# Splitting projection weights one piece further ahead in a two-block transformer kernel

## The reference, cut to what matters

```
u = rmsnorm(h, norm_mix[i]) @ w_mix_in[i]
z, xbc, dt_raw, q, k, v, q_idx, k_idx, w_idx = split(u)
y_ssd = ssd_mixer(z, xbc, dt_raw, ...)      # 16 heads of a state-space mixer
y_att = dsa_mixer(q, k, v, q_idx, k_idx, w_idx, positions)  # 8 heads, top 64 keys of an indexer
h = h + concat(y_ssd, y_att) @ w_mix_out[i]
```

## Time and profile before

| | |
|---|---|
| median of three runs | 2865.03 us |
| the profiled execution | 2873.32 us, its span 2871.5 us |
| PE busy | 2749.1 us, 96% of the span |
| DVE, ACT, POOL busy | 65%, 45%, 14% |
| mean granted TensorE clock | 0.976 of full speed |
| moved by DMA | 445.24 MB, mean 155 GB/s |

### The profile page before, as it was taken

How to read it: one execution, slowest core, us unless ns; L and a number is a source line. 1 busy time by engine, 2 the same in 40 slices (tenths; PEclk the granted TensorE clock), 3 DMA queues, 4 the chain that set the end, 5 groups by cost and what they waited for, 6 DMA issues and landing times.

```text
span 2871.5 us, 40240 instructions
## 1 busy us (share of the span) xinstructions
PE 2749.1 (96%) x17078; PEld 2334.2 (81%) x17078; DVE 1877.0 (65%) x2495; ACT 1284.3 (45%) x1603; POOL 392.3 (14%) x331
## 2 busy tenths in 40 slices
PE   7999998999999999899999999999999979999998
PEld 6889877888888977788888765768878868889787
DVE  7856467685775546678599643347757659654774
ACT  5433535444444344554433544524444433665443
POOL 2400010231230001023004311010000001411000
PEclk9998999999999899999999999999999999999999
DMA  7563694455554479255423221235545524334652
GB/s 230 183 194 108 219 288 154 147 187 188 168 183 155 148 232 298 91 183 186 146 74 101 82 70 61 69 106 188 184 161 183 185 68 147 99 119 126 211 184 96
DMA packets 442329, 445.24 MB, mean 155 GB/s; under 512 B 13711, under 2 KB 433672, under 8 KB 442150
## 3 DMA queue, kind: packets, MB, share of 16 engines
q1 hardware_dynamic: 438878, 436.52, 47.6%
q0 software_dynamic: 2400, 5.40, 0.8%
q10 hardware_dynamic: 872, 0.75, 0.1%
HBM read 441.46 MB, written 1.17 MB: 154 GB/s over the span
## 4 chain that ended last, share of the span: by engine, by line
PE 88%; DVE 7%; ACT 3%; DMA 1%; issue 1%; SPq 0%; ACTq 0%; DVEq 0%
PE bank L1655 30%; PE bank L1617 19%; PE bank L1656 15%; PE bank L1609 7%; PE bank L1754 4%; PE bank L1650 2%; DVE R L2723 2%; PE bank L1871 2%; PE bank L2079 1%; PE bank L1812 1%; PE bank L2070 1%; DVE lower L2230 1%; DVE lower L724 1%; PE bank L1941 1%; ACT upper L1084 1%
## 5 line engine op out<-in xcount | busy, mean ns | idle before, releaser
L1655 PE MATMUL bank<-h_pair,upper 128*128 128x512 f32 x2464 | 877.0, 400 | 31.9 <-DVE h_pair L2263 18.7
L2230 DVE TENSOR_TENSOR lower<-ring,upper 128x2048 fp32r<-128x2048 f32 (+1 forms) x238 | 567.2, 2385 | 291.2 <-ACT upper L1084 291.1
L1656 PE MATMUL bank<-h_pair,lower 128*128 128x256 f32 x2464 | 694.5, 282 | 0.0
L1084 ACT ACTIVATE upper<-ring 128x2048 fp32r<-128x2048 f32 (+1 forms) x238 | 441.7, 1863 | 484.2 <-PE bank L1656 482.9
L1655 PEld LDWEIGHTS bank<-h_pair,upper 128*128 128x128 f32 x2464 | 467.4, 190 | 147.9 <-issue 29.3
L1656 PEld LDWEIGHTS bank<-h_pair,lower 128*128 128x128 f32 x2464 | 470.3, 191 | 0.2
L1655 PE MATMUL bank<-hid_pair,upper 128*128 128x512 f32 x1232 | 432.7, 396 | 0.0
L1656 PE MATMUL bank<-hid_pair,lower 128*128 128x256 f32 x1232 | 344.9, 280 | 0.0
L1655 PEld LDWEIGHTS bank<-hid_pair,upper 128*128 128x128 f32 x1232 | 231.1, 188 | 55.2
L717 DVE TENSOR_TENSOR lower<-ring,upper 128x2048 fp32r<-128x2048 f32 (+1 forms) x68 | 149.2, 2196 | 167.5 <-ACT upper L1050 167.5
L1617 PE MATMUL bank<-h_up,upper 128*128 128x512 f32 (+1 forms) x640 | 227.2, 355 | 20.3 <-DVE h_low L2677 19.0
(11 more groups left out here) (334 smaller groups left out, 4566.1 us busy)
## 6 DMA issues: line engine op xcount, KB each, us to landing
ring<-in_w_ffn_in SPq DMA_DIRECT2D x154, 1024.0 KB, 5.1
ring<-in_w_ffn_out SPq DMA_DIRECT2D x56, 1024.0 KB, 4.9
ring<-in_w_mix_in SPq DMA_DIRECT2D x48, 1024.0 KB, 5.4
ring<-in_w_mod SPq DMA_DIRECT2D x48, 1024.0 KB, 6.7
ring<-in_w_in SPq DMA_DIRECT2D x42, 1024.0 KB, 5.2
ring<-in_w_ffn_out SPq DMA_DIRECT2D x28, 768.0 KB, 4.2
ring<-in_w_mix_out SPq DMA_DIRECT2D x16, 1024.0 KB, 5.8
ring<-in_w_in SPq DMA_DIRECT2D x16, 512.0 KB, 5.2
```

The costliest lines, as they stand in the source:

```text
L1084: act.activation(f.upper(p)[:, 0:n], slot[:, 0:n], ACT.Copy).then_inc(up_ready, 1)
L1655: pe.matmul(bank[:, 0:2 * T], up[:, cols], x_pair.rearrange("p e t -> p (e t)"), start=first, stop=False)
L1656: return pe.matmul(bank[:, 0:T], low[:, cols], x_pair[:, 0, :], start=False, stop=last)
L2230: dve.tensor_tensor(f.lower(p)[:, 0:n], slot[:, 0:n], f.upper(p)[:, 0:n].bitcast(F32), ALU.subtract)\
```

## The change

Uppers and lowers of the qkv pieces are made two pieces ahead instead of one. On ACT piece n + 2 is split right after the result of piece n has been copied out; before, piece n + 1 was split just before waiting for piece n. Piece 1 is now split after the last piece of z. On DVE the lowers follow, and in the pairs they stand on the other side of the decay rows (L2582). The first piece of the output projection is split on ACT before the squares and roots, not between the two roots, and on DVE before the reciprocals, not in attention step 3. What PE and SyncE run, and in which order, stays as it was.

```diff
                     if i == 0:
                         split1_up(mixp + 13)
-                    elif i == 2:
-                        split1_up(poss + FILL_PIECE["qkv", 0])
+                    elif i >= 2:
+                        split1_up(poss + FILL_PIECE["qkv", i - 2])
 
                 def take_fills(kind, i):
                     for what, n in FILLS.get((kind, i), ()):
                         it = items + FILL_ITEM[what, n]
-                        if what == "qkv" and n + 1 < len(QKV_AT):
-                            split1_up(poss + FILL_PIECE[what, n + 1])
                         filled(act, it)
                         if what == "qkv":
                             take_item(it, [(qkv[:, :, PC * n:PC * (n + 1)], token_halves(banks(it)[0]))])
+                            if n + 2 < len(QKV_AT):
+                                split1_up(poss + FILL_PIECE[what, n + 2])
...
+                split1_up(poss + MIXO_PIECE)
                 for gr in range(2):
                     act.wait_ge(y_gated, (l * KD + 4 * (gr + 1)))
...
                                    scale=2.0 / D).then_inc(yroot_ready, 1)
-                    if gr == 0:
-                        split1_up(poss + MIXO_PIECE)
...
                 def qkv_ahead(kind, i):
 
                     for what, n in FILLS.get((kind, i), ()):
-                        if what == "qkv" and n + 1 < len(QKV_AT):
-                            split1_low(dve, poss + FILL_PIECE[what, n + 1])
+                        if what == "qkv" and n + 2 < len(QKV_AT):
+                            split1_low(dve, poss + FILL_PIECE[what, n + 2])
...
-                split1_low(dve, poss + FILL_PIECE["qkv", 0])
+                for n in range(2):
+                    split1_low(dve, poss + FILL_PIECE["qkv", n])
...
-                    qkv_ahead("logit", u)
+                    qkv_ahead("logit", u - 2)
+                qkv_ahead("logit", 6)
+                qkv_ahead("logit", 7)
                 turned_mod("logit", 7)
...
                         ins.then_inc(mt_ready, 1)
-                    qkv_ahead("head", 2 * i - 1)
+                    qkv_ahead("head", 2 * i - 2)
                     if i < PAIRS:
...
                         ins.then_inc(seg_ready, 1)
+                    qkv_ahead("head", 2 * i - 1)
                     for e in range(2):
                         turned_mod("head", 2 * (i - 1) + e)
...
-                    qkv_ahead("head", 2 * i)
                     if i in TOPK_AT_PAIRS:
                         top_round()
...
                 chain.settle()
+                split1_low(dve, poss + MIXO_PIECE)
                 for gr in range(2):
...
-                    elif 3 <= i < ATT_H + 2:
+                    elif 4 <= i < ATT_H + 2:
                         split1_low(dve, poss + MIXO_PIECE + i - 3)
```

## The result

The changed kernel takes 2944.94 us (median of 4 runs, 2938.26 to 2946.3), the kernel before 2863.41 us beside it. The ratio is 1.0273, with a 95% interval of 1.0244 to 1.0303: slower by some 80 us, as predicted in direction and within the range; the forecast was 2935. The profiled execution of the changed kernel, 2953.58 us, is not among the four; the profiled one of the kernel before, 2873.32 us, lies about as far above its median, so that the two can be compared.

The account below looks back on a forecast made before the run. PE was taken to bound the kernel, with work in 96% of the span. Delays of 54 us for two layers plus 16 us of clock on the profiled 2873.3 us gave 2943, against the median 2935 us; range 2900 to 2972.

Parts of the forecast that it names:

- The strain on the ring: Six-slot ring: at distance six, a transfer is issued only when piece n finishes and lands 5.3 to 6.5 us later.
- the term for qkv 3: After qkv 1: ACT's split and DVE's lower of qkv 3 delay PE, 2.4 us per layer, from 0 to 4.
- A: End of z: the split of qkv 1 delays the indexer's copies, 6.0 us per layer.
- B: At qkv 0: the split behind it delays the relu of step 3 that PE needs, 4.7 us per layer.
- rival 2: No change: ACT's idle time around every copy absorbs the waits, 2865 us; chance 0.06.
- E: At qkv 7: the split delays the mod copy that PE's turn needs, 6.1 us per layer.
- F: At qkv 8: the split delays the mod's bank that PE needs for qkv 9, 3.9 us per layer.
- G: At qkv 9: the split delays the mod copy ahead of PE's turn, 5.6 us per layer.
- The output piece: First output piece: 0.2 us lost at the roots, 1.7 us gained in the attention, per layer.
- The clock: Half clock behind new PE gaps: 2.0 us each at four of five gaps, 16 us over the kernel.
- Rival 1: Slower still: landings 2 us longer, full clock price at every gap, 2959 us, with uncosted delays 2973; chance 0.10.
- Rival 3: Faster, at roots and output projection start: early slot refills close gaps, 2857 us, with other waits 2849; chance 0.04.

Follow-up runs that it names:

- the early ones alone: Kernel before with only qkv pieces 1 and 2 split two ahead: 2893.57 us, ratio 1.0101.
- the late ones alone: Kernel before with only qkv pieces 9, 10 and 11 split two ahead: 2913.8 us, ratio 1.0177.
- near pieces, with and without piece 3: Kernel before with only qkv pieces 3 to 8 split two ahead: 2871.29 us, ratio 1.0023; with only 4 to 8: 2865.80 us, ratio 1.0004.
- taking the clock out: Changed kernel with useless matmuls on PE just before each of the five waits of a layer: 2921.6 us, ratio 1.0198 to the kernel before.

## Why the prediction was right, and which term was off

**The mechanism.** Right, and tested from both sides. The strain on the ring was at the five places named: the early ones alone cost 29 us and the late ones alone 49, and neither fits a price per moved piece. Pieces 4 or 5 apart cost nothing but the term for qkv 3 (near pieces, with and without piece 3). That ACT's place in its program decides, the run with the split behind the mod copies shows for the late places; for A and B it is argued from the same pattern in the trace. That run also answers rival 2, which had ACT's idle time absorb the stops: it can, once the short copies go first.

**The gaps.** Place A was predicted as 6.0 on top of 1.8 us and came as 7.90; B 4.7 and 4.69; E 6.1 and 6.39; F 3.9 and 3.93; G 5.6 and 4.83, since its landing took 5.3 us and not the 6.0 of the earlier trace rows. The term after qkv 1 was too large, 2.4 us predicted and 1.29 and 1.28 measured: only the gap at the cumulative sum's copy came, not the one at the turn. In layer 1, where I had the same numbers, B's landing took 7.1 us and its gap was 6.41, and E's landing took 5.5 us and its gap was 5.07; with the early pieces alone B's gap in layer 1 was 4.66, so the 7.1 us belong to this execution. Together I had 54 us for the two layers, and PE's idle time grew by 54.1. That the sum fits so closely is in part luck: terms that came out too large and too small cancel.

**The output piece.** The prediction's 0.2 lost and 1.7 gained was right in the gaps, but the 0.2 is a difference of two: the root's gap did not stay near 2 us, as I had expected to see, but fell to 0.56, and a new one of 2.15 opened ahead of the sums. In time it was not right: measured alone, the edit gave nothing that can be told, and in its trace PE's matmuls behind the new gap ran at a lower clock. I had priced the clock only behind the five large gaps.

**The clock.** This is the term that was mis-sized: 16 us, from four of five gaps at 2.0 us each. PE's busy time grew by 26.2 us over the program, and by 32 us in the two mixers; taking the clock out gave 23 us back. Two things were too small. All ten gaps had a stretch at the lower clock, not eight. And the price of 2.0 came from a single stretch of 4.9 us, where the ten new ones were 6.4 us long in the mean. The share that is lost in such a stretch was nearly right: I had 1 - 26/44 = 0.41, from matmuls counted in windows. The rows behind place B's gap, at the lower clock and then at full clock, begin the same group of three matmuls every 0.64 and every 0.36 us, which is 0.44:

```profile
335.20 0.63 PE L1608 MATMUL bank<-upper,h_pair 128*128 128x256 f32 x2
...
335.84 0.63 PE L1608 MATMUL bank<-upper,h_pair 128*128 128x256 f32 x2
...
338.38 0.40 PE L1608 MATMUL bank<-upper,h_pair 128*128 128x256 f32 x2
...
338.74 0.40 PE L1608 MATMUL bank<-upper,h_pair 128*128 128x256 f32 x2
```

With 64 us at the lower clock that share gives an estimated 28 us, my count of matmuls 26. The penalty as a fixed half of the throttled time, which the prediction quoted from the Trainium skill ("TensorE: Matmul & The Clock Gate", Terms), gives an estimated 32. The 23 to 32 us measured do not decide between them.

**The sum.** 54 + 16 on 2865 gave 2935. With the 26.2 us by which PE's busy time grew in place of the 16 it is 2945, and the median was 2944.94; that last agreement shows nothing new, since in the profiled pair idle and busy time add up to the span by themselves.

**The chances.** They do not add up as written: the forecast and rival 1 (slower) have 0.90 together, where the prediction gave "slower" 0.92, and rival 2 and the small half of rival 3 have 0.08, where it gave "same" 0.06.

**Rival 1** (slower still) had two parts. Longer landings did not come: of the ten, nine took 5.3 to 6.8 us and one 7.1. The full clock price at every gap did.

**Rival 3** (faster) needed landings within 3 us of their issue. In the trace after the shortest of the ten took 5.3 us.

## What to carry to other kernels

Looking one piece further ahead is worth nothing where the splits are never late, and turns into a stop where the piece's slot is the one that has just been emptied. Compare the distance in pieces with the depth of the ring before moving a wait forward. In an engine's program, put the short copies that others need ahead of any wait for a transfer; that alone was worth 44 of 49 us here. And count a new gap on PE with its second price: here about 2.3 us of clock in the mean on top of a gap of 4 to 8 us, with a large spread from one gap to the next.

## What the runs showed of the hardware that was not expected

The clock could be lower behind a gap of 2.15 us as well: the sums behind it took 5.27 to 5.41 us instead of 4.10 in the changed kernel and with the output piece alone. Behind the same gap, with useless matmuls in the stage ahead of it, it stayed at 1.00 and they took 3.72. How long PE then stayed at the lower level did not follow the length of the gap: 3.9 us behind one of 7.63, 9.8 us behind one of 4.83. And useless matmuls in front of a wait made the program 23 us faster, though they add 400 matmuls: the granted clock stayed at 1.00 where idle time had brought it to 0.50.
